# Another order of VectorE's and ScalarE's work behind each norm, and normalised chunks at a pitch of 768

## The chip, the cores and the metric

One core of a Trainium2 chip. The metric is the time of one execution on the device in microseconds; a kernel's time is the median of its runs. Fp32 throughout; the engines are TensorE (PE in profiles), VectorE (DVE), ScalarE (ACT), GpSimd (POOL) and SyncE (SP, which only issues DMAs here).

## What is computed

Two layers of a transformer-like trunk over 512 latent and 256 context tokens of width 1024. Each layer is half a SwiGLU FFN, a mixer (layer 0: neighbourhood attention and a Mamba-2 scan; layer 1: RG-LRU and differential attention), and another half FFN. Ahead of each of the six stages (`n` = 0 to 5) stands a modulated norm:

```python
def _modulate(h, g, m, k):
    return (rms_norm(h, g) * (1 + m[:, :, 3 * k + 1]) + m[:, :, 3 * k]).astype(h.dtype)

def swiglu(h, w1, w3, w2):
    return (jax.nn.silu(h @ w1) * (h @ w3)) @ w2

def _half_ffn(h, g, m, k, w1, w3, w2):
    y = swiglu(_modulate(h, g, m, k), w1, w3, w2)
    return h + (0.5 * m[:, :, 3 * k + 2] * y).astype(h.dtype)
```

Norms 0, 2, 3 and 5 are followed by a half FFN (2816 hidden columns, in two halves of 11 pairs of weight tiles), norms 1 and 4 by the input projection of a mixer. Norm 5 and what follows work on the 512 latent tokens alone.

## The kernel before

**Layout.** Activations lie feature-major: `x[P, 8, 768]`, 8 chunks of 128 features by 768 tokens. Every product is done in three parts with operands split into a rounded high part and a remainder: `wh·xh`, `wh·xl`, `wl·xh` (L450, L452, L454 for 768 tokens in two banks of 384 columns; L457, L459, L461 for pieces of up to 512 columns). `xh`, `xl` are `[P, 8, TX]` with `TX = 784` words from one chunk to the next, `hh`, `hl` (the hidden activations, operands of the down products) `[P, 11, 768]`. Weight tiles alternate between slot 0 and slot 1 (`raw`, `wh`, `wl`, and PSUM `G[0]`, `G[1]`): SP loads `raw` (L366), ScalarE makes `wh` (`split_hi`, L961), VectorE makes `wl` (`split_lo`, L1422), TensorE multiplies. All engines run their own program in written order and meet at semaphores.

**Around a norm.** The last tiles of the stage before (`down`) update `x`. With each updated chunk, `modA·x` is split into the unnormed operand (`hxh`, `hxl` for n = 2 and 5, else in the place of `xh`, `xl`, at 784 words a chunk) and its square is summed. TensorE multiplies the first two weight tiles of the next stage with this unnormed operand (`gemm_unnormed`, L509), so that it works while the norm is made; two columns of shift go along. The reciprocal root `rstd` is applied afterwards to the two banks (`scale_bank`). From the third weight tile on the normalised operand is needed: `gemm_staggered` (L484) takes tile b+2 (slot 0) chunk by chunk and tile b+3 (slot 1) three chunks behind it.

The normalised operand is made in three steps a chunk: VectorE scales into `vn[j % 4]` (L1608; these four buffers are `tmp`), ScalarE adds the shift into `xh` (L1079), VectorE subtracts for `xl` (`rest`, L1599). For n = 1, 3, 4 `xh` lies where the unnormed operand is still read, so ScalarE waits for `u_read` of TensorE. VectorE's order is scaled 0, scaled 1, rest 0, `between(0)`, scaled 2, rest 1, and so on in turn, with `between(1)` behind rest 4. `between(s)` scales bank s and makes `wl` of the third or fourth tile. In norms 1 and 4 that is `scale_tile`. In the gated norms 2, 3 and 5 it is `scale_gate` for bank 0, and `scale_hidden` for bank 1, which also multiplies with the gate, whose Silu ScalarE does behind chunk 3 (`between_up`, L1091). `psum_free[0]`, which slot 0's next tile needs, comes from that Silu; `psum_free[1]` from `scale_hidden`. ScalarE stores the hidden product into `hh` (L1010) behind the norm; in the FFN after norm 2 it then loads `scb`, takes its Silu (`load_scb`, L983) and only then splits the next weight tile.

Of the kernel before, what the change touches and what calls it, by code (L numbers as in the profile page):

```python
# [22 lines left out]
P = 128  # L23
# [3 lines left out]
KC = D // P  # L27
# [52 lines left out]
def build(nc, dr):  # L80
    ctx = ExitStack()
    with ctx:
# [3 lines left out]
        def at(name, shape, word, dt=F32):  # L86
            return nc.alloc_sbuf_tensor_at(name, shape, dt, offset=arena0 + 4 * word)
# [1 line left out]
        w = 0  # L89
        x = at("x", [P, KC, T], w); w += KC * T  # L90
        XH = w
        xh = at("xh", [P, KC, TX], w, F32R); w += KC * TX
        XL = w
        xl = at("xl", [P, KC, TX], w, F32R); w += KC * TX
        H = w
        hh = at("hh", [P, FH, T], w, F32R); w += FH * T
        hl = at("hl", [P, FH, T], w, F32R); w += FH * T
# [235 lines left out]

        def unnormed(n):

            return (hxh, hxl) if n in (2, 5) else (xh, xl)

        def shift(n):

# [95 lines left out]
        def _(pe):  # L435
# [72 lines left out]

            def gemm_unnormed(t, n, segs):  # L509

                uh, ul = (hxh, hxl) if n in (2, 5) else (xh, xl)
                e = NLAT if segs is SEGS else NLAT // 2
                ns = segs[-1][1]
                for s in range(2):
                    weights_ready(t + s, s, t // 2)
                    for k in range(KC):
                        if s == 0:
                            pe.wait_ge(u_ready, 8 * (n - 1) + k + 1)
                        W, L = wh[s][:, k * P:(k + 1) * P], wl[s][:, k * P:(k + 1) * P]
                        parts = ((0, e, 0), (512, 512 + ns + 2 - e, e))  # L520
                        for a, b, o in parts:
                            pe.matmul(G[s][:, a:b], W, uh[:, k, o:o + b - a], start=(k == 0), stop=False)  # L522
                        for a, b, o in parts:
                            pe.matmul(G[s][:, a:b], W, ul[:, k, o:o + b - a], start=False, stop=False)  # L524
                        for a, b, o in parts:
                            mm = pe.matmul(G[s][:, a:b], L, uh[:, k, o:o + b - a], start=False, stop=(k == KC - 1))  # L526
                        if k == KC - 1:
                            mm.then_inc(mm_done, 1)
                        elif s == 1 and n in IN_PLACE:
                            mm.then_inc(u_read, 1)  # L530
                        if s == 0 and k == 2:
                            norm_sums(n, segs)
# [414 lines left out]
        def _(act):  # L947
# [40 lines left out]
            def up(b, hb, look, mods, ns, unnormed_first):  # L988
# [17 lines left out]
                first = 0  # L1006
                if unnormed_first:

                    act.wait_ge(psum_free[1], b // 2 + 1)
                    act.activation(hh[:, 0, 0:ns], hfu[:, 0:ns], ACT.Copy).then_inc(h_hi, 1)  # L1010
                    first = 1
                if mods is None:
# [49 lines left out]
            def norm(n, segs, between):  # L1062
# [6 lines left out]
                for j in range(KC):  # L1069
# [10 lines left out]
                    ins.then_inc(xn_hi, 1)  # L1080
                    between(j)

            def between_tiles(n):
                def between(j):
                    if j == 0:
                        split_hi(FIRST_TILE[n] + 2, 0, FIRST_TILE[n] // 2 + 1, KC)
                    if j == 4:
                        split_hi(FIRST_TILE[n] + 3, 1, FIRST_TILE[n] // 2 + 1, KC)
                return between

            def between_up(n, segs):  # L1091
                def between(j):
                    if j == 0:
                        split_hi(FIRST_TILE[n] + 2, 0, FIRST_TILE[n] // 2 + 1, KC)
                    if j == 3:
                        act.wait_ge(u_gate, LATE_UP.index(n) + 1)
                        for a, b, c in segs:
                            ins = act.activation(g1u[:, a:b], g1u[:, a:b], ACT.Silu, bias=pb[:, 0, c:c + 1])
                        ins.then_inc(psum_free[0], 1)
                    if j == 4:  # L1100
                        split_hi(FIRST_TILE[n] + 3, 1, FIRST_TILE[n] // 2 + 1, KC)
                return between

# [306 lines left out]
        def _(dve):  # L1410
            chained = [0]

            def chain(ins):

                chained[0] += 1
                ins.then_inc(dve_chain, 1)
                dve.wait_ge(dve_chain, chained[0])
# [75 lines left out]
                scale_bank(0, n, segs[-1][1], g1u).then_inc(u_gate, 1)  # L1493
                split_lo(FIRST_TILE[n] + 2, 0, KC)

            def scale_hidden(n, segs):

                chain(scale_bank(1, n, segs[-1][1], hfu))
                dve.wait_ge(psum_free[0], FIRST_TILE[n] // 2 + 1)
                for a, b, c in segs:  # L1500
                    ins = dve.scalar_tensor_tensor(hfu[:, a:b], hfu[:, a:b], pb[:, 1, c:c + 1], g1u[:, a:b], ALU.add, ALU.mult)
                ins.then_inc(psum_free[1], 1)
                split_lo(FIRST_TILE[n] + 3, 1, KC)

            def scale_tile(c, n, out):

# [84 lines left out]
            def norm(n, segs, between):  # L1591
                ns = segs[-1][1]
                c0 = (n // 3) * NMT + 3 * KC * (n % 3)

                def rest(j):
                    dve.wait_ge(v_ready, 8 * n + j + 1)
                    dve.wait_ge(xn_hi, 8 * n + j + 1)
                    for a, b, c in segs:
                        ins = dve.scalar_tensor_tensor(xl[:, j, a:b], vn[j % 4][:, a:b], M[:, c0 + j, c:c + 1],  # L1599
                                                       xh[:, j, a:b].bitcast(F32), ALU.add, ALU.subtract)  # L1600
                    ins.then_inc(xn_ready, 1)

                dve.wait_ge(rstd_ready, n + 1)
                for j in range(KC):
                    if j >= 4:
                        dve.wait_ge(xn_ready, 8 * n + j - 3)
                    for a, b, c in segs:
                        ins = dve.scalar_tensor_tensor(vn[j % 4][:, a:b], x[:, j, a:b], modA[:, n, j, c:c + 1], rstd[:, a:b],  # L1608
                                                       ALU.mult, ALU.mult)
                    ins.then_inc(v_ready, 1)  # L1610
                    if j >= 1:
                        rest(j - 1)
                    if j == 1:
                        between(0)
                    if j == 5:
                        between(1)
                rest(KC - 1)

            def ffn(f, n, base, look, mods, segs, nn=None):
                for h in range(2):  # L1620
# [418 lines left out]
            prep(0)  # L2039
            norm(0, SEGS, lambda s: None)  # L2040
            ffn(0, 0, BASE["ffn0"], KC, 0, SEGS, 1)
            norm(1, SEGS, lambda s: scale_tile(s, 1, vT[:, s, :]))
            ab_in_dve()
            na_dve()
            ssd_dve()
            prep(2)
            down(ABO, KC, KC, 1, SEGS, 2)
            norm(2, SEGS, lambda s: (scale_gate, scale_hidden)[s](2, SEGS))
            ffn(1, 2, BASE["ffn1"], KC, 20, SEGS, 3)
            norm(3, SEGS, lambda s: (scale_gate, scale_hidden)[s](3, SEGS))  # L2050
            ffn(2, 3, BASE["ffn2"], KC, None, SEGS, 4)
            norm(4, SEGS, lambda s: scale_tile(s, 4, vT2[:, s, :]))
            cd_in_dve()
            cd_mid_dve()
            prep(5)
            down(CDO, KC, KC, 4, LSEG, 5)
            norm(5, LSEG, lambda s: (scale_gate, scale_hidden)[s](5, LSEG))
            ffn(3, 5, BASE["ffn3"], 0, None, LSEG)


# [206 lines left out]
```

## Time and profile before

| | |
|---|---|
| median of 3 runs | 3011.83 us (3011.64 to 3012.61) |
| profiled execution | 3014.03 us, span 3012.2 us |
| TensorE busy | 2838.8 us (94%), 15780 matmuls, mean granted clock 0.978 |
| VectorE busy | 1550.5 us (51%) |
| ScalarE busy | 1084.4 us (36%) |
| GpSimd busy | 571.9 us (19%) |
| DMA | 258.77 MB, mean 86 GB/s |

Busy shares are means over the span. A row of a timeline is one instruction, or several alike that were merged (x2); in brackets stands how long its engine had been idle and what it waited for ("issue": for nothing that the profile shows). The granted clock is 1.00 for 2.4 GHz and 0.50 for 1.2 GHz.

### The profile page before, as it was taken

The page shows a single profiled execution, that of the slowest core. Times are in us where ns is not written, and L with a number is a line of the kernel's source. Part 1 is how long each engine was busy: PE and PEld are TensorE (multiplying, and loading weights), DVE is VectorE, ACT ScalarE, POOL GpSimd, SP SyncE. Part 2 cuts the span into 40 slices and gives each one's busy share as a digit, 9 for nine tenths or more (in the row PEclk, how much of TensorE's full clock was granted, in tenths as well). Part 3 has the DMA queues.
Part 4 walks back from the last instruction along what each step waited for, and adds up shares of the span by engine and source line. Part 5 has one row for each costly group of instructions (what it writes and reads, how often), then busy time and mean ns, then how long its engine had stood idle before and what let it go on. Part 6 is the DMA issues. An engine that isn't in the chain of part 4 may idle for free.

```text
span 3012.2 us, 40953 instructions
## 1 busy us (share of the span) xinstructions
PE 2838.8 (94%) x15780; PEld 2645.9 (88%) x15780; DVE 1550.5 (51%) x2035; ACT 1084.4 (36%) x1514; POOL 571.9 (19%) x294
## 2 busy tenths in 40 slices
PE   6999999999977689999999999999999987899999
PEld 5999999988965688999999999999998854688887
DVE  6964366454556856662565532222255557643333
ACT  3432144236445334441343322112224657432221
POOL 2441144100012721440442100000020113200000
PEclk8999999999999999999999999999999989899999
DMA  7343144111210013441442112112211210122232
GB/s 296 132 154 116 59 160 152 65 49 54 71 37 1 1 36 112 153 166 58 133 160 95 45 63 65 67 56 63 73 52 64 62 50 1 43 90 98 91 94 102
DMA packets 67672, 258.77 MB, mean 86 GB/s; under 512 B 7424, under 2 KB 8576, under 8 KB 66944
## 3 DMA queue, kind: packets, MB, share of 16 engines
q1 hardware_dynamic: 50016, 192.58, 19.2%
q10 hardware_dynamic: 17568, 65.02, 6.3%
q8 instruction: 55, 0.90, 0.1%
q14 instruction: 33, 0.27, 0.0%
HBM read 255.47 MB, written 2.10 MB: 86 GB/s over the span
## 4 chain that ended last, share of the span: by engine, by line
PE 85%; DVE 8%; issue 2%; ACT 2%; POOL 1%; DVEq 0%; ACTq 0%; POOLq 0%
PE G L454 21%; PE G L452 21%; PE G L450 20%; PE G L459 5%; PE G L457 5%; PE G L461 5%; DVE B L1427 1%; DVE sL L1813 1%; DVE wl L1422 1%; PE NP L757 1%; PE G L849 1%; PE G L526 1%; PE G L524 1%; PE G L522 1%; PE NP L666 1%
## 5 line engine op out<-in xcount | busy, mean ns | idle before, releaser
L961 ACT ACTIVATE wh<-raw 128x1024 fp32r<-128x1024 f32 (+1 forms) x300 | 338.6, 1129 | 1559.5 <-PE G L454 1244.5
L450 PE MATMUL G<-xh,wh 128*128 128x384 f32 x2624 | 676.3, 339 | 42.1 <-DVE wl L1422 23.9
L454 PE MATMUL G<-xh,wl 128*128 128x384 f32 x2624 | 676.2, 339 | 0.0
L452 PE MATMUL G<-xl,wh 128*128 128x384 f32 x2624 | 676.1, 339 | 0.0
L1422 DVE TENSOR_TENSOR wl<-raw,wh 128x1024 fp32r<-128x1024 f32 (+1 forms) x300 | 426.8, 1423 | 390.9 <-ACT wh L961 390.1
L450 PEld LDWEIGHTS G<-xh,wh 128*128 128x128 f32 x2624 | 478.4, 190 | 49.2 <-DVE wl L1422 22.9
L454 PEld LDWEIGHTS G<-xh,wl 128*128 128x128 f32 x2624 | 481.2, 190 | 0.0
L452 PEld LDWEIGHTS G<-xl,wh 128*128 128x128 f32 x2624 | 477.9, 190 | 0.0
L2078 POOL TENSOR_TENSOR mraw<-mraw,scb 128x1024 f32<-128x1024 f32 x120 | 314.9, 2624 | 648.0 <-DVE B L1427 648.0
L452 PE MATMUL G<-hl,wh 128*128 128x384 f32 x1056 | 268.1, 334 | 0.0
L450 PE MATMUL G<-hh,wh 128*128 128x384 f32 x1056 | 267.8, 334 | 0.0
L454 PE MATMUL G<-hh,wl 128*128 128x384 f32 x1056 | 267.8, 334 | 0.0
L1427 DVE SCALAR_TENSOR_TENSOR B<-mraw,scb 128x1024 f32<-128x1024 f32 x120 | 235.3, 1961 | 0.0
L1525 DVE SCALAR_TENSOR_TENSOR x<-G,modG,x 128x256 f32<-128x256 f32 x112 | 49.1, 480 | 351.1 <-PE G L454 351.1
L1457 DVE TENSOR_TENSOR tmp<-tmp,G 128x768 f32<-128x768 f32 x64 | 61.0, 954 | 286.4 <-PE G L454 286.4
L457 PE MATMUL G<-xh,wh 128*128 128x512 f32 (+1 forms) x528 | 201.9, 392 | 4.4 <-issue 2.5
L459 PE MATMUL G<-xl,wh 128*128 128x512 f32 (+1 forms) x528 | 201.1, 391 | 0.0
L461 PE MATMUL G<-xh,wl 128*128 128x512 f32 (+1 forms) x528 | 200.2, 389 | 0.0
L454 PEld LDWEIGHTS G<-hh,wl 128*128 128x128 f32 x1056 | 190.7, 188 | 0.0
L452 PEld LDWEIGHTS G<-hl,wh 128*128 128x128 f32 x1056 | 190.7, 188 | 0.0
L450 PEld LDWEIGHTS G<-hh,wh 128*128 128x128 f32 x1056 | 190.5, 188 | 0.0
L977 ACT ACTIVATE mraw<-mraw 128x1024 f32<-128x1024 f32 x120 | 126.3, 1052 | 40.7 <-ACT mraw L977 23.6
(332 smaller groups left out, 3259.6 us busy)
## 6 DMA issues: line engine op xcount, KB each, us to landing
raw<-in_w SPq DMA_DIRECT2D x176, 512.0 KB, 3.5
mraw<-in_wmn ACTq DMA_DIRECT2D x120, 512.0 KB, 4.5
raw<-in_w SPq DMA_DIRECT2D x64, 704.0 KB, 4.0
raw<-in_abin SPq DMA_DIRECT2D x24, 512.0 KB, 3.5
raw<-in_cdin SPq DMA_DIRECT2D x20, 512.0 KB, 3.5
mini<-in_wmn SPq DMA_DIRECT2D x9, 512.0 KB, 14.7
gmini<-in_wmn SPq DMA_DIRECT2D x2, 2048.0 KB, 21.7
raw<-in_about SPq DMA_DIRECT2D x8, 512.0 KB, 3.4
```

The lines of the kernel that those rows point to most:

```text
L450: pe.matmul(bank(h), W, tokens(rh, h), start=(k == 0), stop=False)
L452: pe.matmul(bank(h), W, tokens(rl, h), start=False, stop=False)
L454: mm = pe.matmul(bank(h), L, tokens(rh, h), start=False, stop=(k == nk - 1))
L457: pe.matmul(G[slot][:, a:b], W, rh[:, k, a:b], start=(k == 0), stop=False)
L459: pe.matmul(G[slot][:, a:b], W, rl[:, k, a:b], start=False, stop=False)
L461: mm = pe.matmul(G[slot][:, a:b], L, rh[:, k, a:b], start=False, stop=(k == nk - 1))
L961: act.activation(wh[slot][:, 0:nk * P], raw[slot][:, 0:nk * P], ACT.Copy).then_inc(hi_done, 1)
L977: act.activation(mraw[:, j, :], mraw[:, j, :], ACT.Copy, accum_out=M[:, bass.ds(it * 3 + (24 + j), 1), 1:2].rearrange("p a s -> p (a s)")) ...
L1422: dve.tensor_tensor(wl[slot][:, 0:nk * P], raw[slot][:, 0:nk * P], wh[slot][:, 0:nk * P].bitcast(F32), ALU.subtract).then_inc(lo_done, 1)
L1427: return dve.scalar_tensor_tensor(B67[:], tile, 1.0, scv[:, s, :], ALU.mult, ALU.mult, accum_out=out)
L1457: dve.tensor_tensor(by_block(hf[:, 0:T]), by_block(g1s[:, 0:T]), from_banks(G[1], 0, T), ALU.mult).then_inc(psum_free[1], 1)
L2078: pool.tensor_tensor(mraw[:, j, :], mraw[:, j, :], scb[:, 1, :], ALU.mult).then_inc(mod_prod, 1)
```

## The change

Three things change. Normalised chunks of `xh` and `xl` lie 768 words apart; the unnormed operand keeps 784 under the names `uxh`, `uxl`. VectorE's order behind each norm becomes: scaled 0 to 3, `between(0)`, rest 0, rest 1, scaled 4, rest 2, scaled 5, rest 3, `between(1)`, rest 4, scaled 6, rest 5, scaled 7, rest 6, rest 7, `between(2)`. In the gated norms the hidden product is a step of its own (`hidden`) and goes last; `psum_free[1]` comes from the scaling of bank 1 (`scale_up`), and `u_gate` now counts the gate's scaling and the hidden product. ScalarE does the gate's Silu behind chunk 1 instead of 3 and the split of slot 1 behind chunk 3 instead of 4.

```diff
-        xh = at("xh", [P, KC, TX], w, F32R); w += KC * TX
+        xh, uxh = at("xh", [P, KC, T], w, F32R), at("uxh", [P, KC, TX], w, F32R); w += KC * TX
-        xl = at("xl", [P, KC, TX], w, F32R); w += KC * TX
+        xl, uxl = at("xl", [P, KC, T], w, F32R), at("uxl", [P, KC, TX], w, F32R); w += KC * TX
...
         def unnormed(n):
-            return (hxh, hxl) if n in (2, 5) else (xh, xl)
+            return (hxh, hxl) if n in (2, 5) else (uxh, uxl)
...
                 if unnormed_first:
-                    act.wait_ge(psum_free[1], b // 2 + 1)
+                    act.wait_ge(u_gate, 2 * LATE_UP.index(b_norm[b]) + 2)
                     act.activation(hh[:, 0, 0:ns], hfu[:, 0:ns], ACT.Copy).then_inc(h_hi, 1)
...
             def between_tiles(n):
-                    if j == 4:
+                    if j == 3:
                         split_hi(FIRST_TILE[n] + 3, 1, FIRST_TILE[n] // 2 + 1, KC)
...
             def between_up(n, segs):
-                    if j == 3:
-                        act.wait_ge(u_gate, LATE_UP.index(n) + 1)
+                    if j == 1:
+                        act.wait_ge(u_gate, 2 * LATE_UP.index(n) + 1)
                         for a, b, c in segs:
                             ins = act.activation(g1u[:, a:b], g1u[:, a:b], ACT.Silu, bias=pb[:, 0, c:c + 1])
                         ins.then_inc(psum_free[0], 1)
-                    if j == 4:
+                    if j == 3:
                         split_hi(FIRST_TILE[n] + 3, 1, FIRST_TILE[n] // 2 + 1, KC)
...
-            def scale_hidden(n, segs):
-                chain(scale_bank(1, n, segs[-1][1], hfu))
+            def scale_up(n, segs):
+                scale_bank(1, n, segs[-1][1], hfu).then_inc(psum_free[1], 1)
+                split_lo(FIRST_TILE[n] + 3, 1, KC)
+
+            def hidden(n, segs):
+                dve.wait_ge(psum_free[1], FIRST_TILE[n] // 2 + 1)
                 dve.wait_ge(psum_free[0], FIRST_TILE[n] // 2 + 1)
                 for a, b, c in segs:
                     ins = dve.scalar_tensor_tensor(hfu[:, a:b], hfu[:, a:b], pb[:, 1, c:c + 1], g1u[:, a:b], ALU.add, ALU.mult)
-                ins.then_inc(psum_free[1], 1)
-                split_lo(FIRST_TILE[n] + 3, 1, KC)
+                ins.then_inc(u_gate, 1)
...
-                dve.wait_ge(rstd_ready, n + 1)
-                for j in range(KC):
+                def scaled(j):
                     if j >= 4:
                         dve.wait_ge(xn_ready, 8 * n + j - 3)
                     for a, b, c in segs:
                         ins = dve.scalar_tensor_tensor(vn[j % 4][:, a:b], x[:, j, a:b], modA[:, n, j, c:c + 1], rstd[:, a:b],
                                                        ALU.mult, ALU.mult)
                     ins.then_inc(v_ready, 1)
-                    if j >= 1:
-                        rest(j - 1)
-                    if j == 1:
-                        between(0)
-                    if j == 5:
-                        between(1)
-                rest(KC - 1)
+                if n:
+                    dve.wait_ge(u_ready, 8 * n)
+                dve.wait_ge(rstd_ready, n + 1)
+                for j in range(4):
+                    scaled(j)
+                between(0)
+                rest(0)
+                for j in range(1, 4):
+                    rest(j)
+                    if j < 3:
+                        scaled(3 + j)
+                between(1)
+                for j in range(4, KC):
+                    rest(j)
+                    if j < 6:
+                        scaled(2 + j)
+                between(2)
...
-            norm(1, SEGS, lambda s: scale_tile(s, 1, vT[:, s, :]))
+            norm(1, SEGS, lambda s: s < 2 and scale_tile(s, 1, vT[:, s, :]))
...
-            norm(2, SEGS, lambda s: (scale_gate, scale_hidden)[s](2, SEGS))
+            norm(2, SEGS, lambda s: (scale_gate, scale_up, hidden)[s](2, SEGS))
```

## Rows read from the trace of the kernel before

**Rows 1.** Groups by line and form, TensorE: count | busy us, mean ns | idle before, releasers
```profile
L450 PE MATMUL G<-xh,wh 128*128 128x384 f32 x2624 | 676.3, 339 | 42.1 <-DVE wl L1422 23.9 <-DVE xl L1599 12.2 <-issue 6.0
...
L457 PE MATMUL G<-xh,wh 128*128 128x512 f32 x496 | 198.1, 399 | 4.4 <-issue 2.5 <-DVE wl L1422 1.9
...
L457 PE MATMUL G<-hh,wh 128*128 128x512 f32 x176 | 68.5, 389 | 0.0
```

**Rows 2.** Timeline of TensorE, norm 1: start us, us, what [idle before <-releaser]
```profile
653.30 1.01 PE L450 MATMUL G<-xh,wh 128*128 128x384 f32 x2 [3.72 <-DVE wl L1422]
```

**Rows 3.** Timeline of VectorE, norm 1
```profile
633.25 2.21 DVE L1608 SCALAR_TENSOR_TENSOR tmp<-x,modA,rstd 128x512 f32<-128x512 f32 x4 [4.79 <-ACT rstd L1068]
...
637.79 1.15 DVE L1599 SCALAR_TENSOR_TENSOR xl<-tmp,M,xh 128x512 fp32r<-128x512 f32 x2 [2.33 <-ACT xh L1079]
...
638.85 0.15 DVE L1486 COPY few<-G 128x2 f32<-128x2 f32 x1
...
641.77 1.14 DVE L1608 SCALAR_TENSOR_TENSOR tmp<-x,modA,rstd 128x512 f32<-128x512 f32 x2
...
652.02 1.22 DVE L1422 TENSOR_TENSOR wl<-raw,wh 128x1024 fp32r<-128x1024 f32 x1
```

**Rows 4.** Timeline of TensorE, norm 4
```profile
2293.28 1.01 PE L450 MATMUL G<-xh,wh 128*128 128x384 f32 x2 [3.73 <-DVE wl L1422]
```

**Rows 5.** Timelines of norm 3: VectorE, ScalarE, TensorE
```profile
1713.44 2.20 DVE L1608 SCALAR_TENSOR_TENSOR tmp<-x,modA,rstd 128x512 f32<-128x512 f32 x4 [4.78 <-ACT rstd L1068]
...
1725.60 1.28 ACT L1098 ACT_TABLE_LOAD   x1
...
1726.90 1.12 ACT L1098 ACTIVATE sq<-sq,few 128x512 f32<-128x512 f32 x2
...
1728.12 0.98 PE L450 MATMUL G<-xh,wh 128*128 128x384 f32 x2 [4.06 <-issue]
...
1747.49 1.06 ACT L961 ACTIVATE wh<-raw 128x1024 fp32r<-128x1024 f32 x1 [2.43 <-PE G L454]
```

**Rows 6.** Timelines of norm 2: TensorE, ScalarE
```profile
1163.66 0.59 PE L450 MATMUL G<-xh,wh 128*128 128x384 f32 x2 [1.93 <-issue]
...
1181.56 1.91 ACT L986 ACTIVATE scb<-scb 128x2048 f32<-128x2048 f32 x1 [6.84 <-DMA scb<-in_ccb]
...
1185.81 0.61 PE L450 MATMUL G<-xh,wh 128*128 128x384 f32 x2 [3.75 <-DVE wl L1422]
```

**Rows 7.** Timelines of norm 5: VectorE, TensorE, ScalarE
```profile
2644.89 1.42 DVE L1608 SCALAR_TENSOR_TENSOR tmp<-x,modA,rstd 128x512 f32<-128x512 f32 x2 [3.51 <-ACT rstd L1068]
...
2654.00 0.47 PE L457 MATMUL G<-xh,wh 128*128 128x512 f32 x1 [2.52 <-issue]
...
2666.96 1.06 ACT L961 ACTIVATE wh<-raw 128x1024 fp32r<-128x1024 f32 x1 [1.24 <-PE G L461]
```

**Rows 8.** Windows behind norms 1, 4 and 2: stretch, its us, busy us (x) by engine, PEclk, DMA
```profile
651.15:657.98 6.83, 4.68 (x15) 4.68 (x16) 6.59 (x13) 2.24 (x4) 0.00 (x0) 0.50 0.26 77
...
2293.00:2296.30 3.30, 3.02 (x9) 3.02 (x10) 3.30 (x7) 1.12 (x2) 0.00 (x0) 0.50 0.49 140
...
1163.70:1167.00 3.30, 3.30 (x19) 3.30 (x20) 2.79 (x8) 2.84 (x5) 0.00 (x0) 1.00 0.00 0
```

**Rows 9.** Windows of the last half FFN: on `xh` (first), on `hh`
```profile
2860.00:2900.00 40.00, 40.00 (x174) 32.42 (x174) 13.73 (x15) 11.95 (x15) 0.00 (x0) 1.00 0.30 94
...
2790.00:2830.00 40.00, 40.00 (x178) 33.06 (x177) 12.95 (x12) 7.20 (x6) 0.00 (x0) 1.00 0.23 76
```

**Rows 10.** Timeline of TensorE, `xh` then `hh`; each pair 141 rows of x2 apart
```profile
1799.79 0.51 PE L452 MATMUL G<-xl,wh 128*128 128x384 f32 x2
...
1848.83 0.51 PE L452 MATMUL G<-xl,wh 128*128 128x384 f32 x2
...
1910.01 0.51 PE L450 MATMUL G<-hh,wh 128*128 128x384 f32 x2
...
1958.89 0.51 PE L450 MATMUL G<-hh,wh 128*128 128x384 f32 x2
```

More of the change, by code:

```diff
@@ L509, in gemm_unnormed @@
             def gemm_unnormed(t, n, segs):
-                uh, ul = (hxh, hxl) if n in (2, 5) else (xh, xl)
+                uh, ul = unnormed(n)
                 e = NLAT if segs is SEGS else NLAT // 2
@@ L1081, in norm @@
                     between(j)
+            b_norm = {FIRST_TILE[n]: n for n in FIRST_TILE}
             def between_tiles(n):
@@ L2047, in _ @@
             down(ABO, KC, KC, 1, SEGS, 2)
-            norm(2, SEGS, lambda s: (scale_gate, scale_hidden)[s](2, SEGS))
+            norm(2, SEGS, lambda s: (scale_gate, scale_up, hidden)[s](2, SEGS))
             ffn(1, 2, BASE["ffn1"], KC, 20, SEGS, 3)
-            norm(3, SEGS, lambda s: (scale_gate, scale_hidden)[s](3, SEGS))
+            norm(3, SEGS, lambda s: (scale_gate, scale_up, hidden)[s](3, SEGS))
             ffn(2, 3, BASE["ffn2"], KC, None, SEGS, 4)
-            norm(4, SEGS, lambda s: scale_tile(s, 4, vT2[:, s, :]))
+            norm(4, SEGS, lambda s: s < 2 and scale_tile(s, 4, vT2[:, s, :]))
             cd_in_dve()
@@ L2056, in _ @@
             down(CDO, KC, KC, 4, LSEG, 5)
-            norm(5, LSEG, lambda s: (scale_gate, scale_hidden)[s](5, LSEG))
+            norm(5, LSEG, lambda s: (scale_gate, scale_up, hidden)[s](5, LSEG))
             ffn(3, 5, BASE["ffn3"], 0, None, LSEG)
```

## The prediction

> **What bounds the kernel now.** First the table: TensorE is busy for 94% of the span, so only two things can shorten the kernel, idle time of TensorE and the time from one matmul to the next. The view of groups by line says where TensorE stands idle in the large products: 42.1 us ahead of L450, of it 23.9 for a weight remainder (`wl`), 12.2 for an activation remainder (`xl`) and 6.0 for nothing shown, and 4.4 us ahead of L457 [rows 1]. The timelines place 3.72, 3.73, 4.06, 1.93, 3.75 and 2.52 us of this behind norms 1 to 5, 19.7 in all [rows 2, 4 to 7]; most of the rest lies in the first 160 us (start and first mod dots), which the change hardly touches.
>
> Norm 1: TensorE starts the second tile of the staggered pair (slot 1) at 653.30, after 3.72 us of idling, the moment VectorE has finished `wl` of slot 1 (652.02 + 1.22) [rows 2, 3]. VectorE had worked without a break since 637.79; before that it stood for 2.33 us behind ScalarE's `xh`, which waited for the unnormed product to leave chunk 0 [rows 3]. So the chain of VectorE sets slot 1, and the old order leaves 2.33 us in it unused. Norm 4 repeats norm 1 (slot 1 at 2293.28) [rows 4]. In norm 3 TensorE stands 4.06 us and starts slot 0 at 1728.12: the gate's Silu on ScalarE starts at 1726.90 for 1.12 us, behind four normalised chunks and a table load of 1.28 us [rows 5]. Norm 5 is the same with 512 tokens: 2.52 us, start at 2654.00 [rows 7]. Norm 2 has 1.93 us ahead of slot 0, but 3.75 us more at 1185.81, and this one hangs on the `scb` load: its Silu starts at 1181.56 after 6.84 us of waiting for the DMA [rows 6].
>
> Each long stall is paid twice, since the granted clock falls to 0.50 behind it: of 651.15 to 657.98 TensorE works 4.68 us at half speed, of 2293.0 to 2296.3 it is 3.02 us. After the 1.93 us at 1163.66 the clock stayed at 1.00 [rows 6, 8].
>
> **The change, part by part, for each norm.** VectorE's prices: a scaled chunk or a remainder of 768 tokens 1.06 us (638.85 − 637.79), the bank step of a tile 2.92 us (641.77 − 638.85) [rows 3]. In a gated norm a bank step has no bias part (estimated at 0.8 us, some less than a chunk's 1.06), which leaves 2.13 us; the hidden product's 1.06 us move from the second one to the end, behind the last remainder. The old order by these prices: 637.79 + 1.06 + 2.92 + 8 × 1.06 + 2.92 = 653.17, 0.13 us ahead of the matmul at 653.30, so the prices and the 0.13 us to the matmul hold. With 512 tokens the unit is about 0.67 us (two scaled chunks take 1.42 with the last one's tail) [rows 7]; I take the bank steps as 1.9 us, the `wl` part being the same.
>
> *Norms 1 and 4.* New chain from the first scaled chunk to `wl` of slot 1: 4 × 1.06 + 2.92 + 6 × 1.06 (three remainders, two scaled, the fourth remainder) + 2.92 = 16.44 us; 633.25 + 16.44 = 649.7, plus 0.13 = 649.8 against 653.30: **3.5 us**. The 2.33 us of waiting are filled with two scaled chunks, and two scaled-plus-remainder units fewer stand ahead of slot 1. ScalarE's split of slot 1, now one chunk earlier, waits for the end of the unnormed product (about 643.8) with chunks 4 to 7 behind it; chunk 4 is ready at about 646, and its remainder comes only at 649.7, so this hides. Slot 0's matmuls on chunks 0 to 2 run from about 643.7 on without a stall, chunk 3 waits for its remainder (646.8), and then about 1.9 us of idling are left ahead of slot 1. That is about the 1.93 us of row 1163.66, so I take the clock to hold: another 4.68 / 2 = **2.3 us** in norm 1, 3.02 / 2 = **1.5 us** in norm 4. Sum 5.8 + 5.0. Bounds: 3.5 each if the clock falls nevertheless; if it falls later and for longer, about 1.7 less.
>
> *Norm 3.* The Silu moves behind chunk 1. VectorE: 1713.44 + 4 × 1.06 + 1.0 = 1718.7 for the scaled bank 0; ScalarE then has its two chunks and the slot-0 split done at about 1719.8, loads the table (1.28) and ends the Silu at about 1722.2, before the unnormed product ends at 1728.12 − 4.06 − 0.2 = 1723.9. So slot 0 starts without a stall. Slot 1: 1713.44 + 4.24 + 2.13 + 6.36 + 2.14 = 1728.3, plus 0.3 because remainder 2 now waits for its `xh` behind the Silu, plus 0.13 = 1728.8. TensorE needs 12 more steps, six matmuls of 0.174 us each [rows 10] = 1.04 us: end at 1741.3. Before, the pair ended at about 1747.4, just ahead of ScalarE's next split at 1747.49 [rows 5]. **6.1 us**, the clock's fall at 0.5 included. What is late next: the following tile's split and remainder, 2.6 us behind the end of slot 0, which is four steps ahead of the end of slot 1: hidden.
>
> *Norm 5.* 2644.89 + 4 × 0.67 + 1.9 + 6 × 0.67 + 1.9 + 0.13 = 2655.5; 12 steps of 3 × 0.23 = 0.69: end at 2663.8 against 2666.96 − 0.1 [rows 7]: **3.1 us**. The weights of the next tile are ready at 2663.6, so the cover here is just used up.
>
> *Norm 2.* The pair would end some 3 us sooner, by the same chain as in norm 3. But the next tile waits for the split that ScalarE does behind the load and Silu of `scb`, and these start when the first hidden product is stored, behind the last remainder: about 0.3 us earlier than now. So the stall of 3.75 us grows to about 6.5 and the gain goes there. I take **0** (bounds −1.5 for a second half-clock stretch, +1 for an earlier load).
>
> *Norm 0.* The order changes here too: remainder 0 comes 2 × 1.06 us later, TensorE's first tile starts so much later, but the next pair waits for the same kind of `scb` load anyway. 0.3 us gained at most; I take 0.
>
> The added wait on `u_ready` is for VectorE's own last remainder, done 4.8 us before rstd arrives [rows 3]; nothing is behind it. The number of DMAs is unchanged; slot 0's and slot 1's next raw loads start within 3 us of their old times, with SP's queue otherwise empty. Order in sum: 5.8 + 0 + 6.1 + 5.0 + 3.1 = **20.0 us**.
>
> *The pitch.* `xh`, `xl` had 784 words from chunk to chunk, `hh`, `hl` have 768, and the same matmul is slower on the former: 512 columns, 40 us of unbroken work hold 174 matmuls on `xh` and 178 on `hh` [rows 9]. Two of each are parts of neighbours, so 232.6 against 227.3 ns; with the edges counted finer I take 5 ns. With 384 columns: 282 matmuls from 1799.79 to 1848.83 (49.04 us) against 282 from 1910.01 to 1958.89 (48.88 us), 0.57 ns each [rows 10]. VectorE and ScalarE are busier beside the former; but in the timeline the spacing on `xh` follows the chunk number and repeats with every fourth chunk, as the starts do that move on by 784 words (64 bytes modulo 256), while on `hh` all steps are alike. 3 × 496 × 5 ns = 7.4 us and 3 × 2624 × 0.57 ns = 4.5 us [rows 1]: **11.9 us**, all of it in products that TensorE bounds. The bounds: nothing, if the cause is another; above, the durations' own difference (399 − 389 ns [rows 1], 15 us in all) overlaps with the next matmul, so it is the most that could be had of L457 to L461. The unnormed products keep 784.
>
> The Trainium skill says otherwise here: "TensorE: Matmul & The Clock Gate", in "Wait — 56ns, not 53.3ns?", has matmuls follow each other at columns over clock plus some 2.5 ns, with no word of addresses. By it 512 columns take 215.8 ns at any pitch, and the pitch term is 0; the rows have 227 and 232 for one shape, so it doesn't hold as it stands.
>
> **Sum.** The profiled execution took 3014.03 us (span 3012.2). 3014.0 − 20.0 − 11.9 = 2982.1, and the median of the runs is 2.2 below that execution: **2980 us**.
>
> **Rivals.**
> 1. *The pitch is worth nothing* (the steps differ by their 8 instead of 11 chunks, or by what runs beside them): 2980 + 12 = 2992. Against it: 512-column steps differ by 2% under equal loops. By the page's rule above this is the case. Chance 0.15.
> 2. *The order gives only part*: the 1.9 us of idling in norms 1 and 4 drops the clock after all (2 × 1.7), norm 2 gets a second half-clock stretch (1.5), and norm 5's cover fails (1): 2980 + 6 = 2986. For it: 1.9 us is at the edge of what the rows show harmless. Chance 0.2.
> 3. *Equal alignment collides*: at 768 words all chunks of `xh`, `xl` start alike, as do the weight tiles, and TensorE's reads meet each other or VectorE's writes. It would have to cost more than 20.0 us over the 9360 matmuls, 2.1 ns each, to make the kernel slower; at 4 ns it ends at 3011.8 − 20 + 37 = 3029. Against it: `hh` has exactly this pitch and is the faster one. Chance 0.03.
> 4. *The norms' gains are absorbed as in norm 2* by whatever follows, and the pitch too gives little: about 3008, no change. Chance 0.03.
>
> The forecast has 0.59. 0.2% of 3012 us, 6 us, is about what a measurement of this kernel can tell from no change: faster 0.94, same 0.03, slower 0.03. Range: from 2974 (norm 2 gains 1, norm 0 as well, the pitch 16 us instead of 12, one unit of the chain less waiting) to 2993 (rival 1).
>
> **What the profile of the changed kernel would show.** No idle time ahead of slot 0 in norms 2, 3 and 5; about 1.9 us (norms 1, 4), 0.5 to 0.8 (norms 2, 3) and 1.3 (norm 5) ahead of slot 1; granted clock 1.00 through norms 1, 3, 4, 5; a stall of about 6.5 us behind norm 2; 178 instead of 174 matmuls in 40 us of `xh` at 512 columns, equal durations for `xh` and `hh`. I am wrong if the clock still falls at the norms, if slot 1 still waits 3 us or more, or if the count stays at 174.

## The result and the profile after

The changed kernel takes 2983.24 us (median of 4 runs, 2982.09 to 2985.11) against 3012.22 us (4 runs, 3011.64 to 3013.46): ratio 0.9904, 95% interval 0.9887 to 0.9921, 29 us less. Its profiled execution has a span of 2980.8 us, 31.4 us shorter than that of before.

The groups by line and form of TensorE, for [rows 1]:

```profile
L450 PE MATMUL G<-xh,wh 128*128 128x384 f32 x2624 | 673.8, 337 | 34.3 <-DVE wl L1424 21.9 <-DVE xl L1605 12.3
...
L457 PE MATMUL G<-xh,wh 128*128 128x512 f32 x496 | 196.0, 395 | 2.8 <-DVE wl L1424 2.8
...
L457 PE MATMUL G<-hh,wh 128*128 128x512 f32 x176 | 68.5, 389 | 0.0
```

The idle time ahead of L450 is down from 42.1 to 34.3 us, and the part that the profile could not explain ("issue", 6.0) is gone. The mean durations fell from 339 to 337 and from 399 to 395 ns. So there are two gains, idle time and the steps from matmul to matmul.

VectorE's timeline in norm 1, for [rows 3]:

```profile
632.40 4.33 DVE L1613 SCALAR_TENSOR_TENSOR tmp<-x,modA,rstd 128x512 f32<-128x512 f32 x8 [4.85 <-ACT rstd L1068]
636.64 0.15 DVE L1488 COPY few<-G 128x2 f32<-128x2 f32 x1
636.71 1.02 DVE L1490 TENSOR_TENSOR vT<-G,rstd 128x512 f32<-128x512 f32 x2
637.76 0.75 DVE L1517 TENSOR_SCALAR vT<-vT,few 128x512 f32<-128x512 f32 x2
638.42 1.22 DVE L1424 TENSOR_TENSOR wl<-raw,wh 128x1024 fp32r<-128x1024 f32 x1
639.56 2.20 DVE L1605 SCALAR_TENSOR_TENSOR xl<-tmp,M,xh 128x512 fp32r<-128x512 f32 x4
...
647.70 1.22 DVE L1424 TENSOR_TENSOR wl<-raw,wh 128x1024 fp32r<-128x1024 f32 x1
```

The first row has eight instructions, four scaled chunks, where four stood before; remainders 0 and 1 follow bank 0 without a break. The wait of 2.33 us for ScalarE's `xh` no longer exists, because by then VectorE has other work. The `wl` of slot 1 is begun at 647.70 instead of 652.02, counted from the start of the unnormed product (623.29, before 624.21) 24.4 us instead of 27.8.

TensorE's timeline: slot 1 in norm 1, slot 0 and slot 1 in norm 3, slot 1 in norms 4 and 5, for [rows 2, 4, 5, 7]:

```profile
648.96 0.62 PE L450 MATMUL G<-xh,wh 128*128 128x384 f32 x2 [1.57 <-DVE wl L1424]
...
1713.63 0.51 PE L450 MATMUL G<-xh,wh 128*128 128x384 f32 x2
...
1718.57 0.61 PE L450 MATMUL G<-xh,wh 128*128 128x384 f32 x2 [0.61 <-DVE wl L1424]
...
2272.76 0.80 PE L450 MATMUL G<-xh,wh 128*128 128x384 f32 x2 [1.60 <-DVE wl L1424]
...
2631.72 0.50 PE L457 MATMUL G<-xh,wh 128*128 128x512 f32 x1 [0.90 <-DVE wl L1424]
```

Slot 0 starts without idling in norm 3 (1713.63, before 4.06 us). Slot 1 waits 1.57, 0.61, 1.60 and 0.90 us, each time for `wl`.

The granted clock in two windows, for [rows 8] (last three numbers: clock, DMA share, GB/s):

```profile
647.30:653.00 5.70, 4.13 (x24) 3.89 (x24) 5.70 (x11) 1.12 (x2) 0.00 (x0) 1.00 0.28 92
...
2273.50:2276.60 3.10, 3.10 (x12) 3.10 (x11) 3.10 (x7) 1.12 (x2) 0.00 (x0) 0.52 0.48 169
```

Behind norm 1 the clock stays at 1.00. Behind norm 4 it is at half again for nearly the whole window, although the idle time ahead of it (1.60) is as long as in norm 1 (1.57).

Norm 2, ScalarE's store of the first hidden product and the Silu of `scb`, and TensorE's start of the next tile, for [rows 6]:

```profile
1165.01 0.85 ACT L1010 ACTIVATE hh<-sq 128x768 fp32r<-128x768 f32 x1 [2.34 <-DVE sq L1508]
...
1171.76 1.91 ACT L986 ACTIVATE scb<-scb 128x2048 f32<-128x2048 f32 x1 [5.90 <-DMA scb<-in_ccb]
...
1176.01 1.00 PE L450 MATMUL G<-xh,wh 128*128 128x384 f32 x2 [5.80 <-DVE wl L1424]
```

The hidden product is stored at 1165.01, the `scb` load is waited for 5.90 us, and TensorE now stands 5.80 us instead of 3.75.

The step from matmul to matmul: 40 us of 512 columns on `xh`, 40 us on `hh`, and two rows of 384 columns on `xh` that stand 141 rows of two matmuls apart, for [rows 9, 10]:

```profile
2830.00:2870.00 40.00, 40.00 (x179) 33.12 (x178) 13.83 (x16) 12.30 (x16) 0.00 (x0) 1.00 0.31 98
...
2760.00:2800.00 40.00, 40.00 (x178) 33.12 (x178) 12.99 (x12) 7.66 (x6) 0.00 (x0) 1.00 0.23 75
...
1789.84 0.51 PE L452 MATMUL G<-xl,wh 128*128 128x384 f32 x2
...
1838.72 0.51 PE L452 MATMUL G<-xl,wh 128*128 128x384 f32 x2
```

179 and 178 matmuls where 174 and 178 stood, and 48.88 us for 282 matmuls on `xh` where it was 49.04; 48.88 is what `hh` had before.

Stage by stage, from the start of the unnormed product (the first matmul of L522 at that norm) to the first matmul of the tile behind the staggered pair, read from TensorE's timelines:

| norm | before, us | after, us | gain | predicted |
|---|---|---|---|---|
| 1 | 624.21 to 668.12 | 623.29 to 661.65 | 5.6 | 5.8 |
| 2 | 1142.06 to 1185.81 | 1133.24 to 1176.01 | 1.0 | 0 |
| 3 | 1704.40 to 1747.29 | 1694.13 to 1731.25 | 5.8 | 6.1 |
| 4 | 2264.20 to 2307.37 | 2247.09 to 2286.92 | 3.3 | 5.0 |
| 5 | 2638.16 to 2666.76 | 2614.43 to 2640.05 | 3.0 | 3.1 |

That is 18.6 us behind the norms of the 31.4; 12.8 lie elsewhere: 0.9 in the first FFN half, 2.4 and 3.3 in the two mixers, 0.5 and 1.1 in the two FFNs between norms 2 and 4, and 4.8 in the last one, each rounded. Not all of it can be credited to the change: in the kernels below that have this pitch the second mixer takes from 327.3 to 331.1 us (here 327.5), and the granted clock in it differs as well.

### The profile page after: what moved, and what is told of

Same layout as the page of the kernel before. It is cut to its first block, busy times and chain, and to the rows that moved or that the text cites. A ratio compares the mean times of both kernels' runs of the same rounds, so it can differ in the third digit from the quotient of the medians.

```text
span 2980.8 us, 40958 instructions
## 1 busy us (share of the span) xinstructions
PE 2818.3 (95%) x15780; PEld 2631.5 (88%) x15780; DVE 1549.7 (52%) x2035; ACT 1083.2 (36%) x1514; POOL 570.0 (19%) x294
## 4 chain that ended last, share of the span: by engine, by line
PE 83%; DVE 9%; ACT 2%; issue 2%; POOL 1%; DMA 0%; DVEq 0%; ACTq 0%; POOLq 0%
PE G L450 20%; PE G L452 20%; PE G L454 20%; PE G L457 5%; PE G L459 5%; PE G L461 5%; DVE B L1429 1%; DVE tmp L1613 1%; DVE sL L1829 1%; DVE wl L1424 1%; PE NP L757 1%; PE G L849 1%; DVE xl L1605 1%; PE NP L666 1%; DVE sL L1820 0%
## 5 line engine op out<-in xcount | busy, mean ns | idle before, releaser
L450 PE MATMUL G<-xh,wh 128*128 128x384 f32 x2624 | 673.8, 337 | 34.3 <-DVE wl L1424 21.9
L454 PE MATMUL G<-xh,wl 128*128 128x384 f32 x2624 | 669.2, 336 | 0.0
L450 PEld LDWEIGHTS G<-xh,wh 128*128 128x128 f32 x2624 | 474.8, 189 | 40.8 <-DVE wl L1424 19.0
L450 PE MATMUL G<-hh,wh 128*128 128x384 f32 x1056 | 268.0, 334 | 0.0
L450 PEld LDWEIGHTS G<-hh,wh 128*128 128x128 f32 x1056 | 190.7, 188 | 0.0
```

The costliest lines, as they stand in the source:

```text
L450: pe.matmul(bank(h), W, tokens(rh, h), start=(k == 0), stop=False)
L454: mm = pe.matmul(bank(h), L, tokens(rh, h), start=False, stop=(k == nk - 1))
```

## The experiments

Times are medians. Kernels that ran on one chip in one go shared the runs of before: e1 to e4 3012.78 us, e5 to e8 3013.66, e9 and e10 3014.24, e11 and e12 3011.89.

**e1_pitch**, the kernel before with the pitch alone:

```diff
-        xh = at("xh", [P, KC, TX], w, F32R); w += KC * TX
+        xh, uxh = at("xh", [P, KC, T], w, F32R), at("uxh", [P, KC, TX], w, F32R); w += KC * TX
```

(`xl` likewise, and the unnormed operand reads `uxh`, `uxl`.)

> The kernel before with the pitch alone: normalised chunks at 768 words, order as before. Theory (two separate gains): the steps of 512 columns on xh fall from 232 to 227 ns and those of 384 columns from 173.9 to 173.3, 11.9 us less than before, about 3000 us; the stalls behind the norms (3.7 us ahead of slot 1 in norms 1 and 4, 4.1 in norm 3, 2.5 in norm 5) stay. Rival (the new order gives everything, the shorter steps are a by-product of it): within 3 us of before.

Measured: 3001.25 us, ratio 0.996 (0.9947 to 0.9974), 11.5 us less. A window of 40 us at 512 columns, slot 1 in norm 1, slot 0 in norm 3:

```profile
2850.00:2890.00 40.00, 40.00 (x178) 33.12 (x178) 13.74 (x15) 11.66 (x15) 0.00 (x0) 1.00 0.32 101
...
651.82 1.01 PE L450 MATMUL G<-xh,wh 128*128 128x384 f32 x2 [3.72 <-DVE wl L1422]
...
1725.73 0.98 PE L450 MATMUL G<-xh,wh 128*128 128x384 f32 x2 [4.06 <-issue]
```

178 matmuls, and the stalls of 3.72 and 4.06 us are those of before. The pitch has its gain by itself.

**e2_order**, the changed kernel with normalised chunks back at 784 words:

```diff
-        xh, uxh = at("xh", [P, KC, T], w, F32R), ...
+        xh, uxh = at("xh", [P, KC, TX], w, F32R), ...
```

> The changed kernel with its normalised chunks back at 784 words. Theory: order alone, 18 to 20 us less than before, about 2993 us; stalls as in the changed kernel (1.7 us ahead of slot 1 in norms 1 and 4, none ahead of slot 0 in norms 3 and 5), 174 matmuls of 512 columns in 40 us. Rival (the two depend on each other): less than 15 us faster than before.

Measured: 2996.11 us, ratio 0.9942 (0.9928 to 0.9955), 16.7 us less; its span is 18.8 us under that of before. The same window, slot 1 in norm 1, and the granted clock behind slot 1's start in norms 1 and 4:

```profile
2840.00:2880.00 40.00, 40.00 (x174) 32.45 (x174) 13.74 (x15) 11.13 (x14) 0.00 (x0) 1.00 0.32 100
...
648.67 0.83 PE L450 MATMUL G<-xh,wh 128*128 128x384 f32 x2 [1.61 <-DVE wl L1424]
...
648.90:652.30 3.40, 3.40 (x12) 3.40 (x12) 3.40 (x7) 1.12 (x2) 0.00 (x0) 0.50 0.48 154
...
2278.60:2282.00 3.40, 3.40 (x19) 3.30 (x20) 3.40 (x7) 1.12 (x2) 0.00 (x0) 1.00 0.51 154
```

174 matmuls again, and the short stall of the new order. Here the clock fell behind norm 1 and held behind norm 4, the other way round than in the changed kernel, at equal idle times (1.61 and 1.60 us). 11.5 and 16.7 make 28.2 of 29.0 us: within what the intervals allow (some 4 us each way) the two add up, and neither needs the other.

The steps also tell what the chunks' starts do. In the last FFN half of this run the mean step of 512 columns is 230.0, 232.8, 232.2 and 231.7 ns for chunks 0 to 3 and 230.1, 232.7, 232.2 and 231.7 for chunks 4 to 7: it repeats with every fourth chunk, that is every 4 × 64 = 256 bytes of shift. In e1_pitch it is 226.6 to 226.8 ns for every chunk.

**e3_shift**, all normalised chunks moved by 64 bytes, pitch 768 kept:

```diff
-        xh, uxh = at("xh", [P, KC, T], w, F32R), ...
+        xh, uxh = at("xh", [P, KC, T], w + 16, F32R), ...
```

> The changed kernel with xh and xl moved on by 16 words (64 bytes), still 768 words from chunk to chunk, so every chunk starts alike but none where the changed kernel has it. Theory A (what costs is that starts change from chunk to chunk): 2983 us as the changed kernel, 178 matmuls in 40 us. Theory B (what costs is a start off a multiple of 256 bytes): steps as long as at 784 words or longer, 12 to 16 us over the changed kernel, about 2995 to 2999.

Measured: 2988.11 us, ratio 0.9914 (0.9899 to 0.9929), 4.9 us over the changed kernel's median; the intervals of the two ratios overlap. 512 columns in 40 us, and 282 matmuls of 384 columns:

```profile
2840.00:2880.00 40.00, 40.00 (x177) 32.81 (x176) 12.46 (x14) 11.05 (x14) 0.00 (x0) 1.00 0.31 96
...
1790.11 0.51 PE L452 MATMUL G<-xl,wh 128*128 128x384 f32 x2
...
1838.99 0.51 PE L452 MATMUL G<-xl,wh 128*128 128x384 f32 x2
```

Neither theory as it stood. Steps of 384 columns are as short as at the original place (48.88 us), as theory A had it. Of 512 columns 177 fit into 40 us, 229 ns each in the timeline, between 227 and 232: at 512 columns the place counts too. Over 1488 matmuls that is some 3 us of the 7.2 us by which the span is over the changed kernel's. The two mixers together took 6.5 us longer and the first FFN half 1.7 us less, which was not traced to a cause.

**e4_pitch776**, chunks 776 words apart:

```diff
-        xh, uxh = at("xh", [P, KC, T], w, F32R), ...
+        xh, uxh = at("xh", [P, KC, T + 8], w, F32R), ...
```

> The changed kernel with normalised chunks 776 words apart (starts move by 32 bytes modulo 256 from chunk to chunk instead of 64 or 0). Theory A (changing starts cost) and theory B (starts off a multiple of 256 bytes cost) both give steps of 231 to 233 ns at 512 columns and some 12 us over the changed kernel; if only steps of 64 bytes are bad, 227 ns and 2983 us.

Measured: 3004.66 us (one run), span 3002.9. The same two readings:

```profile
2840.00:2880.00 40.00, 40.00 (x174) 32.34 (x173) 13.77 (x16) 12.07 (x16) 0.00 (x0) 1.00 0.29 92
...
1789.99 0.51 PE L452 MATMUL G<-xl,wh 128*128 128x384 f32 x2
...
1839.43 0.51 PE L452 MATMUL G<-xl,wh 128*128 128x384 f32 x2
```

174 matmuls in 40 us, as at 784 words, and 49.44 us for 282 of 384 columns, 175.3 ns each, more than the 173.9 at 784. A pitch only 8 words off the best one costs 22 us of span in this one run, where the expectation had 12; by the steps it would be some 24 (1488 × 5.8 ns and 7872 × 2.0 ns), so the miss is the 384 columns, for which 776 is worse than 784. So it isn't that smaller is better: what 768 has and the others lack is that every chunk starts alike modulo 256 bytes, and there at a multiple of it.

**e5_scb**, where norm 2's gain went. ScalarE's split and bank Silu come between the issue of the `scb` load and the wait for it:

```diff
+                def half(i, nk):
+                    split_hi(i * 2 + (b + 2), 0, i + (b // 2 + 1), nk)
+                    ...
+                    act.activation(up_out, up_in, ACT.Silu).then_inc(psum_free[0], 1)
...
-                    load_scb(2)
+                    load_scb(2, lambda: half(1, KC))
```

> The changed kernel; in the FFN after norm 2 ScalarE issues the scb load as before, but does the split of the next slot-0 tile and the Silu that frees its bank before it waits for scb. Theory (the gain of norm 2 went into the wait for scb): the 6.0 us ahead of the fifth tile, and the half-clock stretch behind it, go; 7 to 8 us less than the changed kernel, about 2975.5. Rival (VectorE's mod dots or the later split of slot 1, not ScalarE's order, hold TensorE there): the stall moves one tile on, within 2 us of the changed kernel.

Measured: 2974.79 us, ratio 0.9873 (0.9857 to 0.989), 8.4 us under the changed kernel. ScalarE's split, bank Silu and `scb` Silu, and the only later row in which TensorE idled:

```profile
1165.77 1.06 ACT L961 ACTIVATE wh<-raw 128x1024 fp32r<-128x1024 f32 x1 [1.47 <-DVE hl L1485]
...
1166.73 0.79 ACT L997 ACTIVATE tmp<-G 128x768 f32<-128x768 f32 x1
...
1170.23 1.92 ACT L988 ACTIVATE scb<-scb 128x2048 f32<-128x2048 f32 x1 [2.70 <-DMA scb<-in_ccb]
...
1177.39 0.62 PE L450 MATMUL G<-xh,wh 128*128 128x384 f32 x2 [0.42 <-DVE wl L1430]
```

The split starts at 1165.77, ahead of the Silu of `scb` (1170.23). The stall of 5.80 us is gone, and 0.42 us come back one tile later. Norm 2's stage takes 36.80 us instead of the changed kernel's 42.77, and the FFN behind it, now without half clock, 1.6 us less. The theory holds.

**e6_silu**, the gate's Silu back behind chunk 3:

```diff
-                    if j == 1:
+                    if j == 3:
                         act.wait_ge(u_gate, 2 * LATE_UP.index(n) + 1)
```

> The changed kernel with the gate's Silu back behind chunk 3. Theory (with four scaled chunks made first, ScalarE gets through four chunks early enough anyway): slot 0 in norms 3 and 5 starts at most 0.5 us late, 0 to 1.5 us over the changed kernel, about 2984. Rival (the early Silu is what lets slot 0 start): 3 to 4 us of stall again in norm 3 and 2.5 in norm 5, clock at half behind them, 6 to 9 us more, about 2991.

Measured: 2982.64 us, ratio 0.9897 (0.9881 to 0.9914): no different from the changed kernel. Slot 0 in norm 3:

```profile
1714.04 0.58 PE L450 MATMUL G<-xh,wh 128*128 128x384 f32 x2 [0.34 <-issue]
```

0.34 us of idling ahead of slot 0, and it costs nothing, since slot 1 has to wait for VectorE's `wl` anyway: norm 3's stage takes 36.93 us (37.13 in the changed kernel), norm 5's 25.63 in both.

**e7_turns**, VectorE's old turns, all else as in the changed kernel:

```diff
-                for j in range(4):
-                    scaled(j)
-                between(0)
-                ...
+                for j in range(KC):
+                    scaled(j)
+                    if j >= 1:
+                        rest(j - 1)
+                    if j == 1:
+                        between(0)
+                    if j == 5:
+                        between(1)
+                rest(KC - 1)
                 between(2)
```

> The changed kernel with VectorE's old turns (two scaled chunks, remainder 0, bank 0, then scaled and remainder in turn, bank 1 behind remainder 4); early Silu, hidden product last and pitch 768 stay. Theory (VectorE's chain sets slot 1): stalls of 3.7 us ahead of slot 1 in norms 1 and 4, about 4 in norm 3 and 2 in norm 5, clock at half behind them: 14 to 18 us over the changed kernel, about 2999. Rival (the gain of the gated norms comes from the Silu and the hidden product's place, and only norms 1 and 4 need the turns): 9 to 11 us more, about 2993.

Measured: 3002.55 us, ratio 0.9964 (0.9949 to 0.9978), 19 us over the changed kernel, somewhat more than the 14 to 18 expected. Of the 18.6 us between the spans 16.0 lie behind the norms; the second mixer took 3.6 us longer (331.1 against 327.5, at a mean granted clock of 0.92 against 0.94), and nothing ties that to the order. Slot 1 in norms 1, 3 and 5:

```profile
651.62 1.01 PE L450 MATMUL G<-xh,wh 128*128 128x384 f32 x2 [3.71 <-DVE wl L1424]
...
1726.74 0.62 PE L450 MATMUL G<-xh,wh 128*128 128x384 f32 x2 [2.91 <-DVE wl L1424]
...
2650.39 0.50 PE L457 MATMUL G<-xh,wh 128*128 128x512 f32 x1 [2.18 <-DVE wl L1424]
```

In norm 3 slot 0 starts on time thanks to the early Silu, and 2.91 us of stall simply move to slot 1. In norm 5 it is different: slot 1 waits 2.18 us, but the stage takes 26.55 us, where e1_pitch, with the same pitch and all else as before, needs 28.21. So there the early Silu and the late hidden product are worth 1.7 us by themselves.

**e10_four**, the counterpart, the kernel before with VectorE's order alone:

```diff
+                for j in range(4):
+                    scaled(j)
+                between(0)
+                rest(0)
+                ...
```

(`between(1)` is still `scale_hidden`, the Silu behind chunk 3, the pitch 784.)

> The kernel before with nothing but VectorE's order of scaled chunks and remainders changed: pitch 784, Silu behind chunk 3, hidden product inside the second bank step. Theory (the order of VectorE is the whole of the gain behind the norms): 2 to 3 us less gain than the order part of the change (the hidden product adds 1.1 us ahead of slot 1 in norm 3, 0.7 in norm 5), so about 15 us under before, 2998. Rival (the three parts are needed together in the gated norms): under 11 us, only norms 1 and 4 gain.

Measured: 2997.20 us, ratio 0.9949 (0.9936 to 0.9963), 17.0 us less. Slots 0 and 1 in norm 3:

```profile
1717.25 0.59 PE L450 MATMUL G<-xh,wh 128*128 128x384 f32 x2 [0.34 <-issue]
...
1722.66 0.62 PE L450 MATMUL G<-xh,wh 128*128 128x384 f32 x2 [1.00 <-DVE wl L1422]
```

In norm 3 the order does most of it: slot 0 idles 0.34 us and slot 1 1.00 instead of 0.61. Against e2_order (0.9942) the totals can't tell whether the Silu's and the hidden product's new places are worth anything. The traces can: with them (e2_order) norm 3's stage takes 37.20 us and norm 5's 25.76, without them 38.12 and 26.56, so they are worth 0.9 and 0.8 us, much as the expectation had it.

**e8_halves**, one step on, against the rest of the stall ahead of slot 1:

```diff
                 between(0)
-                rest(0)
-                for j in range(1, 4):
+                for j in range(4):
                     rest(j)
-                    if j < 3:
-                        scaled(3 + j)
                 between(1)
+                for j in range(4, 6):
+                    scaled(j)
...
-                for i in range(KC + lag):
-                    for s, k in ((0, i), (1, i - lag)):
+                    for s, k in [(0, 0), (0, 1), (0, 2), (0, 3), (1, 0), (1, 1), (1, 2), (1, 3), (0, 4), (1, 4), (0, 5), (1, 5),
+                                 (0, 6), (0, 7), (1, 6), (1, 7)]:
```

> The changed kernel one step on: behind remainder 3 the second bank at once, scaled 4 and 5 only after it; TensorE takes chunks 0 to 3 of slot 1 straight behind those of slot 0, then the rest in turn. Theory (what is left ahead of slot 1 is VectorE's two early scaled chunks): 1.7 us less in norms 1 and 4, 0.8 in norm 3, about 1 in norm 5, and no half clock behind norm 4 (1.7): 5 to 7 us less, about 2977. Rival (TensorE then waits as long for remainders 4 and 5): within 2 us of the changed kernel.

Measured: 2978.71 us, ratio 0.9881 (0.9864 to 0.9897), 4.5 us under the changed kernel, but its four runs spread over 7 us (2975.92 to 2983.17) and the profiled one is the slowest of them. The next tile behind norm 1 and behind norm 2:

```profile
658.46 0.62 PE L450 MATMUL G<-xh,wh 128*128 128x384 f32 x2 [0.39 <-DVE wl L1423]
...
1175.89 1.00 PE L450 MATMUL G<-xh,wh 128*128 128x384 f32 x2 [8.42 <-DVE wl L1423]
```

There is no idling ahead of slot 1 in norms 1, 3 and 4 any more, only 0.39 us behind the pair; the stages of norms 1 and 4 take 36.71 us each (38.36 and 39.83 in the changed kernel). Norm 2's stall grows to 8.42 us and its stage from 42.77 to 44.73: the first hidden product is stored no sooner (32.2 us behind the start of the unnormed product, 31.8 in the changed kernel), so what is gained ahead of the `scb` load is waited off behind it, and the load itself took 6.4 us from issue to Silu instead of 4.9, for which no cause was found.

**e9_all**, e5 and e8 together, and the same step after norm 0 (`load_scb(1, lambda: half(0, KC))`):

> The changed kernel with both steps on: ScalarE's split and bank Silu ahead of the wait for scb (after norm 2 and, new, after norm 0), and bank 1 at once behind remainder 3 with chunks 0 to 3 of slot 1 taken together. Theory (the two gains add up, and the 2.6 us that the second lost in norm 2's wait come free): 8.4 + 4.5 + 2 and some 2 to 3 us after norm 0, about 2966. Rival (the earlier arrival is again eaten by the next wait, for VectorE's mod dots or the next tile's weights): no better than the scb step alone, 2972 to 2975.

Measured: 2973.80 us (2970.01 to 2975.25), ratio 0.987 (0.9855 to 0.9885). By the median that is e5's time, the rival's case. The rival's reason does not show, though: in the profiled run, at 2970.01 the fastest of the four, norm 2's stall is down to 0.7 us, and the five stages at norms 1 to 5, measured as in the table above, take 172.7 us together, 3.6 less than in e5, so no later wait has eaten e8's gains. The step after norm 0 brings nothing that can be seen: norm 1's unnormed product starts at 622.97, and in the kernels of this pitch without that step it starts between 621.48 and 623.29.

**e11_two** is e9 without the step after norm 0, and **e12_scb_again** is e5's kernel beside it:

> Both steps without the one after norm 0 (the split ahead of scb stays in the FFN after norm 2 alone; bank 1 at once behind remainder 3). Theory (the step after norm 0 cost about 2 us in the first FFN half and hid the rest): 3 to 4 us under the scb step alone on the same chip, about 2971. Rival (what the second step gains is lost in the spread of the clock's half-speed stretches in the mixers): within 2 us of it.

> The scb step alone once more, as the measure for the kernel beside it on the same chip: 2973 to 2976 us, all of norm 2's gain kept.

Measured: 2971.81 us (2969.84 to 2974.21), ratio 0.9866 (0.9849 to 0.9882), and 2976.14 us (2975.15 to 2978.61), ratio 0.988 (0.9864 to 0.9897). The second step is worth 4.3 us beside the first by the medians, and 3.6 us in the five stages of the traces (172.7 against 176.3); the two intervals overlap, but no run of the one is as slow as the fastest of the other. e11_two is the fastest version, 40 us under the kernel before and 11 under the changed one. That the step after norm 0 costs anything is not shown: e9 and e11 ran on different chips and differ by 2 us, which is inside their spreads, and norm 1's unnormed product starts at 622.52 in e11_two, only 0.45 us sooner than in e9_all.

## Why the prediction was right

**The size.** 2980 us predicted, 2983.24 measured, inside the range. The order was put at 20.0 us and alone gave 16.7 (18.8 in span), the pitch at 11.9 and alone gave 11.5 (10.8 in span). Between the two profiled executions the sum was 31.9 us and 31.4 were measured. Most of what the forecast is off by came at the end: it took the median as 2.2 us below the profiled execution, as before, while the changed kernel's profiled execution (2982.56) happened to lie 0.7 below its median.

**Norms 1 and 3** came within 0.3 us of the sums, and e7_turns and e10_four show the mechanism: VectorE's chain, whose waiting time four scaled chunks fill, sets slot 1. The chain of 16.44 us was 647.70 + 1.22 − 632.40 = 16.52, and TensorE started 16.56 us behind the first scaled chunk, where the prediction had 16.44 + 0.13.

**Norm 4** is the step that failed: "I take the clock to hold". The remaining idle time was 1.60 us, less than the 1.9 estimated and less than the 1.93 that had been harmless, and the clock fell all the same, which is one of the signs that the prediction gave for being wrong. It held behind norm 4 in e2, e5 and e6 at an idle time of that length (their norm 4 took 38.4 us against 39.8 in the changed kernel), while in e2_order it fell behind norm 1 (39.93 us against 38.36). So whether it falls is not a matter of the length alone, and with one trace for each kernel it is open whether norm 4 loses the clock in every execution of the changed one. The 1.7 us lost here stood in rival 2.

**Norm 2** was right in mechanism (the gain goes into the wait for `scb`), shown by e5_scb, and off by 1.0 us in size. The store of the first hidden product comes 1165.01 − 1133.24 = 31.8 us behind the start of the unnormed product, as late as before (1173.88 − 1142.06; I had 0.3 us of gain there); but the load is waited for 5.90 instead of 6.84 us. That is the time of the load itself: from its issue to the Silu of `scb` it took 4.9 us here, 5.8 in the kernel before, 6.9 in e1_pitch and 6.8 in e10_four. With the hidden product last it was 4.8 to 5.1 us in e2, e3, e4, e6 and e7 too, but 6.4 in e8_halves; why was not traced. So TensorE stood 5.80 us and not the 6.5 foretold. The stall's price came later: behind it the clock was at half for 5 us (0.52 from 1176.01 to 1181.00) instead of 3.4 (0.51 from 1187.00 to 1190.40), and the FFN there gained 0.5 us where the same tiles behind norm 3 gained 1.1.

**The parts credited wrongly.** For norms 3 and 5 I named the Silu, moved behind chunk 1, as what frees slot 0. e6_silu shows that with four scaled chunks made first ScalarE gets through chunk 3 soon enough: the place of the Silu is worth 0.34 us of idling in norm 3 and nothing in the total. The sum was right since either edit suffices for slot 0. What is left of the Silu's and the hidden product's new places beside the order is 0.9 us in norm 3 and 0.8 in norm 5, ahead of slot 1 (e2_order against e10_four). In norm 3 the order carries the gain (4.8 of 5.8 us in e10_four). In norm 5 the two overlap: the order alone gives 2.0 us there, the other edits alone 1.7 (e7_turns against e1_pitch), all edits together with the pitch 3.0.

**Norm 0** behaved as foretold: the first tile starts 2.0 us later (57.40 against 55.38), the next pair at 79.76 against 79.75.

**The pitch.** Where TensorE alone sets the pace the term can be read off: 0.57 ns × 1920 matmuls of 384 columns make 1.1 us in the FFN behind norm 3, and 5 ns × 960 of 512 columns make 4.8 us in the last one; 1.1 and 4.8 were measured, in e1_pitch as in the changed kernel. Rival 1 (worth nothing) is out by e1_pitch and e2_order. By the Trainium skill's rule ("TensorE: Matmul & The Clock Gate", "Wait — 56ns, not 53.3ns?") it would have been the case; the rule has no term for the operand's address, and the step here was 226.7 to 232.5 ns (means over the last FFN half in the timelines) for one shape as the starts of the chunks changed. Rival 3 (equal starts collide) is out by the same runs. Rival 4 held for norm 2 alone.

## What to carry to other kernels

Where one engine makes operands for another in turns, look for the wait inside its chain, and fill it with work that needs nothing new, here the scaled chunks; moves on other engines may then be worth little. Give chunks of a moving fp32 operand a pitch that is a multiple of 256 bytes, and start them at one; of such pitches the runs have one, 3072 bytes, and the 256 is read from the steps that repeat with every fourth chunk at 3136. Before a stage is shortened, look for the fixed wait behind it (here a load that is issued and awaited by the engine which also splits the next weights): what is gained ahead of it is lost there, until the work is moved between issue and wait.

## What the runs showed of the hardware

- The step between matmuls depends on where the moving operand starts. 512 columns of fp32 (tiles of type fp32r), granted clock 1.00: 226.7 ns with all chunks at a multiple of 256 bytes, 229 with all of them 64 bytes past one, 232 with starts that move on by 64 bytes, the same 174 per 40 us with 32. 384 columns in three blocks of 128: 173.3, 173.3, 173.9 and 175.3 ns. Why the 384 columns don't mind the uniform shift is open.
- An idle time of TensorE of about 1.6 us can be followed by half clock or not. Ahead of slot 1 in norms 1 and 4 the eight kernels with the new order (the changed one, e2 to e6, e10 and e12) have 16 idle times of 1.57 to 1.61 us; the granted clock fell to 0.50 behind three of them (norm 4 in the changed kernel and in e3_shift, norm 1 in e2_order). It didn't behind 1.93 us in the kernel before and in e1_pitch, and it did behind all six of 3.7 us (norms 1 and 4 in the kernel before, e1_pitch and e7_turns).
